# Attention in pairs of heads: one unit of two heads instead of one, with shared small operations

## The chip, the cores and the metric

The kernel runs on one core of one Trainium2 chip. The metric is the device time of one execution in microseconds, taken as the median of several runs. Lower is better.

## The reference

Two transformer blocks of two layers each, batch 1, 256 tokens, width 1024, all in fp32. The first block has four SwiGLU feed-forwards, an HGRN2 mixer and a forgetting attention of 16 heads. The second has a native sparse attention and a latent attention (12 heads each, plus 4 heads that look at 256 memory rows) and two mixtures of 16 experts. The change touches the attention of three stages, whose core is this, for each head:

```
# forgetting attention ("Fox"), scale = 1/sqrt(64), c = cumsum of log f
s = einsum('bhqd,bhkd->bhqk', qi, k) * scale + cqi[..., None] - c[:, :, None, :]
s = where(key_pos[None, :] <= qpos[:, None], s, MASK_VALUE)
o = einsum('bhqk,bhkd->bhqd', softmax(s), v)          # then o * sigmoid(g) @ w_out
# sparse attention ("Nsa"): o = gate0 * compressed + gate1 * selected + gate2 * window
# latent attention ("Mla"): heads of 64 + 32 columns in q and k, 64 in v, causal
# memory heads (in both): softmax(q mem_k^T / 8) mem_v, not masked
```

With 256 tokens the selected blocks and the window of the sparse attention are both the whole causal range, so each of its 12 heads has two causal softmaxes.

## The kernel before

Each engine's program is written out by hand, stage by stage, and the engines meet only at semaphores. The order of the stages is: FFN, HGRN2, FFN, FFN, Fox, FFN, Nsa, layer norm, mixture of experts, layer norm, Mla, layer norm, mixture of experts, layer norm. Weights come through a ring of three slots of 3 MB. Feed-forwards, projections and experts split each fp32 operand into two fp32r parts and multiply three times; attention multiplies in plain fp32, which the trace records as two records per matmul.

Class `Attention` (from line 1222) is shared by Fox, Nsa and Mla. Its piece of work is a **unit**: one head (in Nsa, one of the two softmaxes of one head) with all 256 queries in two tiles of 128. Fox has 16 units, Nsa 24 and 4 memory units, Mla 12 and 4. A causal unit has 256 keys for the second tile and 128 for the first, so 384 columns of scores; a memory unit has 512. The steps of a unit:

- `pe_score` (L1274): the scores of both tiles into one of four PSUM banks that go round (`banks.claim`). Fox adds a small fp32r product with the decay (`bias_rows`). The contraction is over 64 partitions, 0-63 for an even head and 64-127 for an odd one, and over 96 in Mla.
- `dve_score` (L1366): VectorE adds the mask, negates and takes the row extreme, from PSUM to one of four buffers `pr`.
- `act_units` (L1330): ScalarE makes the exponential of each tile in place, with its row sum.
- `dve_weight` (L1378): reciprocal of the sums, in Nsa times the gate, then one `tensor_scalar` per tile.
- `pe_turn` (L1283): TensorE transposes each 128x128 block of weights into PSUM bank 0 or 1, by turns.
- the copy (`copy_in`, L1318): ScalarE, or VectorE for every fourth unit (`copied_by_dve`, L1315), brings the turned weights to one of four buffers `pt` in the tile named squares.
- `pe_value` (L1298): times the values, 64 output partitions in bank 2 or 3, upper or lower half by the head.
- `dve_quarter` (L1396): after four heads, the bank goes to `cat`.

The order is a software pipeline with lags. At step s TensorE does scores s, turn s-2, values s-4; ScalarE the copy of s-3 and then the exponentials of s; VectorE reads the scores of s, weighs s-1, and copies s-3 if that is its own. The turn of unit g waits for the copy of unit g-2, whose bank it takes:

```
        if g >= 2:
            pe.wait_ge(k.att_copied[g % 2], g // 2)
        pe.wait_ge(k.att_scaled, g + 1)
```

In Nsa, `pe_before` (L1996) starts each pair of heads with one product over the compressed keys (L2008).

Of the kernel before, what the change touches and what calls it, by code (L numbers as in the profile page):

```python
# [24 lines left out]
P = 128  # L25
# [174 lines left out]
class Core:  # L200

    def __init__(self, ctx, nc, a):
# [63 lines left out]
        self.att_copied = [s("att_copied_0"), s("att_copied_1")]  # L267
        self.att_units = 0
        self.att_cols = f32("att_cols", [P, 3, 8])
# [952 lines left out]
class Attention(Mixer):  # L1222
# [6 lines left out]
    TURN_LAG, COPY_LAG, VALUE_LAG, DEEP = 2, 3, 4, 4  # L1229

    def plan_units(self, name, units, at):

        k, n = self.k, len(units)
        self.units, self.u0, self.name = units, k.att_units, name
        k.att_units += n
        part = lambda t: t.rearrange("p (r t) -> p r t", r=self.DEEP)
        self.pr, self.pt = part(at), part(k.sq[:].rearrange("p k t -> p (k t)"))
        self.quarter_end = [max(i for i, u in enumerate(units) if u["head"] // 4 == q) for q in range(4)]  # L1240
        self.quarter_start = [min(i for i, u in enumerate(units) if u["head"] // 4 == q) for q in range(4)]
        for i in range(n):
            k.banks.plan(f"{name}_s{i}")
# [19 lines left out]
    def pe_units(self, pe):  # L1263
        n = len(self.units)
# [33 lines left out]
    def pe_value(self, pe, j):  # L1298
        k, u, g = self.k, self.units[j], self.u0 + j
        q = u["head"] // 4  # L1300
# [17 lines left out]
    def copy_in(self, eng, j):  # L1318

        k, u, g = self.k, self.units[j], self.u0 + j  # L1320
        w = len(u["blocks"]) * P
# [8 lines left out]
    def act_units(self, act):  # L1330
        k, b, n = self.k, self.k.banks, len(self.units)
        for step in range(n + self.COPY_LAG):
            j = step - self.COPY_LAG
            self.act_before(act, step)
            if 0 <= j < n and not self.copied_by_dve(j):
                out, src, copied = self.copy_in(act, j)
                act.activation(out, src, ACT.Copy).then_inc(copied, 1)
            if step < n:
                u, r, c = self.units[step], step % self.DEEP, 2 * ((self.u0 + step) % 4)
                b.wait_read(act, f"{self.name}_s{step}")  # L1340
                for t, at, w in self.tiles(u):
                    e = self.pr[:, r, at:at + w]
                    act.activation(e, e, ACT.Exp, scale=-1.0, bias=k.att_cols[:, 0, c + t:c + t + 1],
                                   accum_out=k.att_cols[:, 1, c + t:c + t + 1]).then_inc(k.att_exp, 1)
        self.act_pieces(act, self.in_pieces + PIECES)

    def dve_units(self, dve):
        n, q = len(self.units), 0
        for step in range(n + self.COPY_LAG):
# [5 lines left out]
            if 0 <= j < n and self.copied_by_dve(j):  # L1355
                out, src, copied = self.copy_in(dve, j)
                dve.tensor_copy(out, src).then_inc(copied, 1)
# [8 lines left out]
    def dve_score(self, dve, i):  # L1366

        k, u, g, r, name = self.k, self.units[i], self.u0 + i, i % self.DEEP, f"{self.name}_s{i}"
        c = 2 * (g % 4)
        if i >= self.DEEP:  # L1370
            dve.wait_ge(k.att_turned, g + 1 - self.DEEP)
        src = k.banks.wait(dve, name)
        for t, at, w in self.tiles(u):
            ins = dve.tensor_tensor_reduce(self.pr[:, r, at:at + w], src[:, at:at + w], u["masks"][t], -u["scale"], -NEG_BIG, ALU.add,
                                           ALU.min, k.att_cols[:, 0, c + t:c + t + 1])
        k.banks.read(ins, name)

    def dve_weight(self, dve, j):  # L1378

        k, seq, u, g = self.k, self.k.dve_seq, self.units[j], self.u0 + j  # L1380
        c = 2 * (g % 4)
        total, weight = k.att_cols[:, 1, c:c + 2], k.att_cols[:, 2, c:c + 2]
# [1557 lines left out]
```

## Time and profile before

| | us |
|---|---|
| median of 3 runs | 2356.04 (2354.56 to 2358.23) |
| the profiled execution | 2355.3 |
| its span | 2353.2 |
| TensorE busy | 2178.4 (93%) |
| VectorE busy | 1527.5 (65%) |
| ScalarE busy | 1179.1 (50%) |
| mean granted TensorE clock | 0.952 of full speed |

### The profile page before, as it was taken

To read this page: it belongs to the slowest core of one execution; us is meant where nothing else is said; L and a number is where in the kernel's file an instruction comes from. 1 tells how busy PE (TensorE), PEld (TensorE's weight loads), DVE (VectorE), ACT (ScalarE), POOL (GpSimd) and SP (SyncE) were. 2 spreads that over 40 slices of the span, in tenths; PEclk is the share of its full clock that TensorE was granted. 3 is DMA by queue.
4 is the path that set the end of the run, shared out by engine and by line. 5 is a ranking of instruction groups with operands and counts; after the bars stand their busy time and mean duration, and the time that the engine had idled before them with its cause. 6 is when DMAs were issued, how large, how long until landed. Compare 5 with 4: busy or idle time off the path is not lost.

```text
span 2353.2 us, 36563 instructions
## 1 busy us (share of the span) xinstructions
PE 2178.4 (93%) x13974; PEld 1935.7 (82%) x13978; DVE 1527.5 (65%) x2373; ACT 1179.1 (50%) x1687; POOL 75.1 (3%) x55
## 2 busy tenths in 40 slices
PE   7998977999999989999999999799999898899997
PEld 6998966999999968779998876687788756778876
DVE  5665668666666544346564446589888455888985
ACT  4443543544434335435443335477776445676774
POOL 1000033000000010000000000000000000000000
PEclk9999998999999999769999969899999999899999
DMA  8545330454455532315545510489996513699991
GB/s 279 199 160 161 112 139 1 164 204 168 161 175 200 161 107 72 127 49 181 200 160 152 159 50 19 143 294 355 312 323 232 206 36 108 215 317 327 319 349 62
DMA packets 312312, 421.09 MB, mean 179 GB/s; under 512 B 7845, under 2 KB 266305, under 8 KB 312097
## 3 DMA queue, kind: packets, MB, share of 16 engines
q1 hardware_dynamic: 308864, 415.93, 52.1%
q10 hardware_dynamic: 2816, 2.38, 0.4%
q0 software_dynamic: 544, 1.62, 0.2%
q8 instruction: 54, 0.88, 0.2%
q14 instruction: 34, 0.27, 0.0%
HBM read 416.69 MB, written 1.05 MB: 178 GB/s over the span
## 4 chain that ended last, share of the span: by engine, by line
PE 84%; DVE 10%; ACT 3%; issue 2%; DMA 1%; ACTq 1%; POOL 0%; DVEq 0%; SPq 0%
PE banks L553 11%; PE banks L555 11%; PE banks L554 11%; PE banks L2493 7%; PE banks L2495 7%; PE banks L2494 7%; PE banks L805 5%; PE banks L806 4%; PE banks L807 4%; PE banks L1280 2%; PE banks L1310 2%; PE banks L2488 2%; PE banks L1289 1%; PE banks L2547 1%; DVE w_lo L2762 1%
## 5 line engine op out<-in xcount | busy, mean ns | idle before, releaser
L2762 DVE TENSOR_TENSOR w_lo<-weight_ring,w_hi 128x1024 fp32r<-128x1024 f32 x384 | 450.1, 1220 | 54.5 <-ACT w_hi L2607 51.1
L553 PE MATMUL banks<-x_hi,w_hi 128*128 128x256 f32 x1408 | 400.6, 284 | 9.0 <-DVE w_lo L506 8.3
L554 PE MATMUL banks<-x_lo,w_hi 128*128 128x256 f32 x1408 | 398.9, 283 | 0.0
L555 PE MATMUL banks<-x_hi,w_lo 128*128 128x256 f32 x1408 | 398.9, 283 | 0.0
L2607 ACT ACTIVATE w_hi<-weight_ring 128x1024 fp32r<-128x1024 f32 x384 | 381.4, 1052 | 33.8 <-PE banks L2495 33.8
L499 ACT ACTIVATE w_hi<-weight_ring 128x1024 fp32r<-128x1024 f32 x88 | 93.0, 1057 | 418.1 <-PE banks L555 418.0
L871 DVE TENSOR_TENSOR pieces<-weight_ring,pieces 128x512 fp32r<-128x512 f32 (+2 forms) x245 | 165.5, 687 | 191.6 <-ACT pieces L860 189.9
L553 PEld LDWEIGHTS banks<-x_hi,w_hi 128*128 128x128 f32 x1408 | 270.8, 192 | 11.3 <-DVE w_lo L506 9.1
L554 PEld LDWEIGHTS banks<-x_lo,w_hi 128*128 128x128 f32 x1408 | 270.9, 192 | 0.1
L555 PEld LDWEIGHTS banks<-x_hi,w_lo 128*128 128x128 f32 x1408 | 270.8, 192 | 0.0
L805 PE MATMUL banks<-split,pieces 128*128 128x256 f32 (+1 forms) x816 | 240.9, 295 | 28.0 <-DVE pieces L871 18.4
L860 ACT ACTIVATE pieces<-weight_ring 128x512 fp32r<-128x512 f32 (+2 forms) x245 | 150.7, 627 | 227.5 <-PE banks L807 217.1
L515 DVE TENSOR_TENSOR w_lo<-weight_ring,w_hi 128x1024 fp32r<-128x1024 f32 x88 | 107.8, 1225 | 240.1 <-ACT w_hi L499 240.1
L806 PE MATMUL banks<-split,pieces 128*128 128x256 f32 (+1 forms) x816 | 236.1, 289 | 0.0
L807 PE MATMUL banks<-split,pieces 128*128 128x256 f32 (+1 forms) x816 | 235.7, 289 | 0.0
L506 DVE TENSOR_TENSOR w_lo<-weight_ring,w_hi 128x2048 fp32r<-128x2048 f32 x88 | 201.2, 2286 | 22.2 <-ACT w_hi L495 21.9
L2493 PE MATMUL banks<-w_hi,x_hi 128*128 128x512 f32 x512 | 207.5, 405 | 2.0 <-ACT wide L2578 2.0
L2495 PE MATMUL banks<-w_lo,x_hi 128*128 128x512 f32 x512 | 201.7, 394 | 0.0
L2494 PE MATMUL banks<-w_hi,x_lo 128*128 128x512 f32 x512 | 200.9, 392 | 0.0
L553 PE MATMUL banks<-h_hi,w_hi 128*128 128x256 f32 x704 | 199.2, 283 | 0.0
L554 PE MATMUL banks<-h_lo,w_hi 128*128 128x256 f32 x704 | 199.2, 283 | 0.0
L555 PE MATMUL banks<-h_hi,w_lo 128*128 128x256 f32 x704 | 199.2, 283 | 0.0
(384 smaller groups left out, 4116.9 us busy)
## 6 DMA issues: line engine op xcount, KB each, us to landing
weight_ring<-in_ffn_w_in SPq DMA_DIRECT2D x88, 1024.0 KB, 7.5
weight_ring<-in_moe_w_gate SPq DMA_DIRECT2D x64, 1024.0 KB, 6.5
weight_ring<-in_moe_w_up SPq DMA_DIRECT2D x64, 1024.0 KB, 9.2
weight_ring<-in_moe_w_down SPq DMA_DIRECT2D x64, 1024.0 KB, 11.1
weight_ring<-in_ffn_w_out SPq DMA_DIRECT2D x44, 1024.0 KB, 9.7
weight_ring<-in_hg_w_in SPq DMA_DIRECT2D x12, 1024.0 KB, 8.3
weight_ring<-in_fox_w_in SPq DMA_DIRECT2D x12, 1024.0 KB, 8.4
weight_ring<-in_nsa_w_in SPq DMA_DIRECT2D x10, 1024.0 KB, 8.0
```

What stands on the lines that cost most here:

```text
L506: dve.tensor_tensor(k.w_lo[:, b, 0:2048].rearrange("p (k n) -> p k n", n=P), raw[:, 0:4096].rearrange("p (k n) -> p k n", n=256)[:, :, jj ...
L553: pe.matmul(out, w_hi, m_hi, start=start, stop=False, skip_group_check=True)
L554: pe.matmul(out, w_hi, m_lo, start=False, stop=False, skip_group_check=True)
L555: return pe.matmul(out, w_lo, m_hi, start=False, stop=stop, skip_group_check=True)
L805: pe.matmul(out, l_hi, r_hi, start=start, stop=False, skip_group_check=True)
L806: pe.matmul(out, l_hi, r_lo, start=False, stop=False, skip_group_check=True)
L807: return pe.matmul(out, l_lo, r_hi, start=False, stop=stop, skip_group_check=True)
L2493: pe.matmul(out, m_hi, w_hi, start=start, stop=False, skip_group_check=True)
L2494: pe.matmul(out, m_lo, w_hi, start=False, stop=False, skip_group_check=True)
L2495: return pe.matmul(out, m_hi, w_lo, start=False, stop=stop, skip_group_check=True)
L2607: act.activation(self.piece(s, p, self.w_hi), self.piece(s, p), ACT.Copy).then_inc(sem[kind + "_hi"], 1)
L2762: dve.tensor_tensor(self.piece(s, p, self.w_lo), self.piece(s, p), self.piece(s, p, self.w_hi.bitcast(F32)), ALU.subtract).then_inc(sem[ki ...
```

## The change

A unit becomes a pair of heads, the even one on partitions 0-63 and the odd one on 64-127. In Nsa a pair is the same softmax of two neighbouring heads, so its units are listed in another order. There are 8 pairs in Fox, 14 in Nsa, 8 in Mla.

- `pe_score` takes two banks and alternates the two heads' matmuls; `pe_value` alternates them too.
- `pe_turn` fills banks 0 and 1 with one pair and waits for the copy of the pair before it. There are no longer two banks by turns.
- One copy moves both heads, 2x384 or 2x512 elements. `pt` has two buffers of a pair in place of four of a unit, `pr` four of a pair (two of them in the first half of the tile wide).
- One reciprocal, one gate multiplication and one multiply per tile serve both heads. The multiply is a `tensor_tensor` with the weights broadcast along the row, in place of `tensor_scalar`.
- Values lag by 3 steps, not 4. ScalarE waits for the last turn before it goes on to the output projection's pieces.

```diff
-    TURN_LAG, COPY_LAG, VALUE_LAG, DEEP = 2, 3, 4, 4
+    TURN_LAG, COPY_LAG, VALUE_LAG, DEEP = 2, 3, 3, 4
...
     def pe_score(self, pe, i):
-        u, name = self.units[i], f"{self.name}_s{i}"
-        out = self.k.banks.claim(pe, name)
-        for t, at, n in self.tiles(u):
-            pairs = u["scores"][t]
-            for m, (left, right) in enumerate(pairs):
-                last = pe.matmul(out[:, at:at + n], left, right, start=m == 0, stop=m == len(pairs) - 1)
-        self.k.banks.filled(last, name)
+
+        k, pair = self.k, self.pairs[i]
+        outs = [k.banks.claim(pe, f"{self.name}_s{i}_{half}") for half in range(2)]
+        last = [None, None]
+        for t, at, n in self.tiles(pair[0]):
+            count = len(pair[0]["scores"][t])
+            for m in range(count):
+                for half in range(2):
+                    left, right = pair[half]["scores"][t][m]
+                    last[half] = pe.matmul(outs[half][:, at:at + n], left, right, start=m == 0, stop=m == count - 1)
+        for half in range(2):
+            k.banks.filled(last[half], f"{self.name}_s{i}_{half}")
 
     def pe_turn(self, pe, j):
-        k, u, g = self.k, self.units[j], self.u0 + j
-        if g >= 2:
-            pe.wait_ge(k.att_copied[g % 2], g // 2)
+        k, g = self.k, self.u0 + j
         pe.wait_ge(k.att_scaled, g + 1)
-        for m, (t, at) in enumerate(u["blocks"]):
-            last = pe.transpose(k.psum[:, g % 2, m * P:(m + 1) * P], self.pr[:, j % self.DEEP, at:at + P], k.ident)
+        if g:
+            pe.wait_ge(k.att_copied, g)
+        for half in range(2):
+            for m, (t, at) in enumerate(self.pairs[j][half]["blocks"]):
+                last = pe.transpose(k.psum[:, half, m * P:(m + 1) * P], self.pr[j % self.DEEP][:, half, at:at + P], k.ident)
         last.then_inc(k.att_turned, 1)
...
-        pe.wait_ge(k.att_copied[g % 2], g // 2 + 1)
-        half = u["head"] % 2 * HD
-        out = k.psum[half:half + HD, 2 + q % 2, u["head"] % 4 // 2 * T:(u["head"] % 4 // 2 + 1) * T]
+        pe.wait_ge(k.att_copied, g + 1)
+        out = k.psum[:, 2 + q % 2, head % 4 // 2 * T:(head % 4 // 2 + 1) * T]
         at = 0
-        for m, v in enumerate(u["values"]):
-            first, n = (T - u["spans"][m], u["spans"][m])
-            last = pe.matmul(out[:, first:T], v, self.pt[:, j % self.DEEP, at:at + n], start=m == 0 and u["first"],
-                             stop=m == len(u["values"]) - 1, skip_group_check=True)
+        for m, n in enumerate(pair[0]["spans"]):
+            for half in range(2):
+                last = pe.matmul(out[half * HD:(half + 1) * HD, T - n:T], pair[half]["values"][m], self.pt[:, j % 2, half, at:at + n],
+                                 start=m == 0 and pair[half]["first"], stop=m == len(pair[0]["spans"]) - 1, skip_group_check=True)
...
-        if j >= self.DEEP:
-            eng.wait_ge(k.att_out, g + 1 - self.DEEP)
-        return self.pt[:, j % self.DEEP, 0:w], k.psum[:, g % 2, 0:w], k.att_copied[g % 2]
+        if j >= 2:
+            eng.wait_ge(k.att_out, g - 1)
+        return self.pt[:, j % 2, :, 0:w], k.psum[:, 0:2, 0:w]
...
-        for t, at, w in self.tiles(u):
-            e = self.pr[:, j % self.DEEP, at:at + w]
-            ins = dve.tensor_scalar(e, e, k.att_cols[:, 2, c + t:c + t + 1], None, ALU.mult)
+        for t, at, w in self.tiles(pair[0]):
+            e = self.pr[j % self.DEEP][:, :, at:at + w]
+            ins = dve.tensor_tensor(e, e, weight[:, t].unsqueeze(2).to_broadcast([P, 2, w]), ALU.mult)
```

TensorE in the middle of Fox, before: one step. The arena operands are the heads' queries and keys, squares the turned weights.

```order
L1280 MATMUL banks<-arena 128x256 [waits bank_free_0]
L1280 MATMUL banks<-bias_rows 128x256
L1280 MATMUL banks<-arena 128x128
L1280 MATMUL banks<-bias_rows 128x128
L1289 MATMUL banks<-consts,arena 128x128 [waits att_scaled,att_copied_1]
L1289 MATMUL banks<-consts,arena 128x128 x2
L1310 MATMUL banks<-squares,arena 64x256 [waits att_copied_1]
L1310 MATMUL banks<-squares,arena 64x128
```

The same place in the changed kernel:

```order
L1288 MATMUL banks<-arena 128x256 [waits bank_free_2,bank_free_1]
L1288 MATMUL banks<-arena 128x256
L1288 MATMUL banks<-bias_rows 128x256 x2
L1288 MATMUL banks<-arena 128x128 x2
L1288 MATMUL banks<-bias_rows 128x128 x2
L1299 MATMUL banks<-consts,wide 128x128 [waits att_copied,att_scaled]
L1299 MATMUL banks<-consts,wide 128x128 x5
L1320 MATMUL banks<-squares,arena 64x256 [waits att_copied]
L1320 MATMUL banks<-squares,arena 64x256
L1320 MATMUL banks<-squares,arena 64x128 x2
```

A step holds two heads, and the turn waits on one semaphore that counts every copy, where it waited on the count of its own bank.

VectorE in Fox before, around the first copy that is its own (L1357): the copy of unit 3 stands between the multiply of unit 5 and the read of unit 7.

```order
L1374 ISA arena,att_cols<-banks,consts 128x256 [waits bank_ready_1,att_turned]
L1374 ISA att_cols 128x1
L1374 ISA arena,att_cols<-banks,consts 128x128
L1374 ISA att_cols 128x1
L1385 RECIPROCAL att_cols<-att_cols 128x2 [waits att_exp]
L1393 TENSOR_SCALAR arena<-arena,att_cols 128x256 [waits dve_seq]
L1393 TENSOR_SCALAR arena<-arena,att_cols 128x128
L1357 COPY squares<-banks 128x384 [waits att_turned]
```

And in the changed kernel, where the copy of pair 3 (L1369) stands behind the read of pair 6 and the multiply of pair 5:

```order
L1388 ISA wide,att_cols<-banks,consts 128x256 [waits bank_ready_3,att_turned]
L1388 ISA att_cols 128x1
L1388 ISA wide,att_cols<-banks,consts 128x128
L1388 ISA att_cols 128x1
L1388 ISA wide,att_cols<-banks,consts 128x256 [waits bank_ready_0]
L1388 ISA att_cols 128x1
L1388 ISA wide,att_cols<-banks,consts 128x128
L1388 ISA att_cols 128x1
L1399 RECIPROCAL att_cols<-att_cols 128x4 [waits att_exp]
L1407 TENSOR_TENSOR arena<-arena,att_cols 128x2x256 [waits dve_seq]
L1407 TENSOR_TENSOR arena<-arena,att_cols 128x2x128
L1369 COPY squares<-banks 128x2x384 [waits att_out,att_turned]
```

The position is the same, but what stands ahead of the copy is twice as much.

## Rows read from the trace of the kernel before

**Rows 1.** Windows, Fox, Nsa, Mla: length; PE, PEld, DVE, ACT, POOL busy; clock; DMA; GB/s.
```profile
974.74:1037.22 62.48, 61.02 (x208) 41.46 (x208) 25.21 (x121) 24.62 (x83) 0.00 (x0) 0.54 0.11 39
1382.46:1455.10 72.64, 70.54 (x328) 46.41 (x328) 48.93 (x239) 41.25 (x143) 0.00 (x0) 0.89 0.00 1
1914.80:1950.61 35.81, 33.73 (x180) 22.84 (x180) 26.26 (x122) 24.94 (x83) 0.00 (x0) 1.00 0.19 59
```
**Rows 2.** The chain that ended last, Fox: start us, us, what.
```profile
1007.21 1.90 PE banks L1280 x6
1009.10 0.83 PE banks L1289 x3
1009.93 1.47 PE banks L1310 x4
```
**Rows 3.** The same chain in Nsa, and the scores of a head in Mla.
```profile
1406.67 0.85 PE banks L1280 x4
1407.52 0.48 PE banks L1289 x3
1408.00 0.80 PE banks L1310 x4
...
1932.40 0.85 PE banks L1280 x4
```
**Rows 4.** Chain (first row), then timeline of TensorE: Fox's start, Mla's last values.
```profile
974.74 1.11 PE banks L1280 x6
...
976.62 0.30 PE L1280 MATMUL banks<-bias_rows 64*128 64x128 f32 x1
978.38 0.90 PE L1289 MATMUL banks<-consts,arena 128*128 128x128 f32 x3 [1.46 <-DVE arena L1393]
...
1947.07 1.08 PE L1310 MATMUL banks<-squares,arena 128*64 128x256 f32 x4
1948.67 1.94 PE L1310 MATMUL banks<-squares,arena 128*64 128x256 f32 x12
```
**Rows 5.** Timeline of a unit in Nsa: start us, us, engine, line, operation.
```profile
1437.07 0.42 DVE L1374 CUSTOM_DVE_ANT_0 arena<-banks,consts 128x256 f32<-128x256 f32 x1 [0.62 <-PE banks L1280]
1437.63 0.16 DVE L1387 RECIPROCAL att_cols<-att_cols 128x2 f32<-128x2 f32 x1
1438.02 0.55 DVE L1393 TENSOR_SCALAR arena<-arena,att_cols 128x256 f32<-128x256 f32 x2
1438.12 0.92 PE L1280 MATMUL banks<-arena 64*128 64x256 f32 x4
1439.18 0.42 DVE L1374 CUSTOM_DVE_ANT_0 arena<-banks,consts 128x256 f32<-128x256 f32 x1 [0.15 <-PE banks L1280]
1439.87 0.51 ACT L1343 ACTIVATE arena<-arena,att_cols 128x256 f32<-128x256 f32 x1 [0.76 <-DVE att_cols L1374]
1440.76 0.47 ACT L1337 ACTIVATE squares<-banks 128x384 f32<-128x384 f32 x1
```
**Rows 6.** Groups of instructions by shape, whole span: busy us, mean ns of one.
```profile
L871 DVE TENSOR_TENSOR pieces<-weight_ring,pieces 128x512 fp32r<-128x512 f32 x242 | 163.9, 689 | 188.7 <-ACT pieces L860 187.0
L529 DVE TENSOR_TENSOR slot_out<-banks,rstd 128x256 f32<-128x256 f32 x176 | 66.4, 419 | 21.0 <-PE banks L555 14.2
L1393 DVE TENSOR_SCALAR arena<-arena,att_cols 128x256 f32<-128x256 f32 x68 | 23.3, 352 | 2.1
L1393 DVE TENSOR_SCALAR arena<-arena,att_cols 128x128 f32<-128x128 f32 x52 | 14.6, 280 | 0.0
L1404 DVE COPY wide<-banks 128x512 f32<-128x512 f32 x8 | 5.5, 683 | 0.0
```
**Rows 7.** Windows behind Fox's last turns; columns as in rows 1.
```profile
1035.00:1037.00 2.00, 2.00 (x15) 1.23 (x13) 1.42 (x3) 1.88 (x4) 0.00 (x0) 0.76 0.00 0
1037.00:1039.00 2.00, 0.22 (x2) 0.00 (x0) 2.00 (x4) 0.42 (x1) 0.00 (x0) 1.00 0.00 0
1039.00:1042.00 3.00, 2.71 (x13) 2.74 (x14) 1.95 (x4) 0.21 (x1) 0.00 (x0) 0.56 0.00 0
```

More of the change, by code:

```diff
@@ L1263, in pe_units @@
     def pe_units(self, pe):
-        n = len(self.units)
+        n = len(self.pairs)
         for step in range(n + self.VALUE_LAG):
@@ L1298, in pe_value @@
     def pe_value(self, pe, j):
-        k, u, g = self.k, self.units[j], self.u0 + j
-        q = u["head"] // 4
+        k, pair, g = self.k, self.pairs[j], self.u0 + j
+        head = pair[0]["head"]
+        q = head // 4
         if q >= 2 and j == self.quarter_start[q]:
@@ L1330, in act_units @@
     def act_units(self, act):
-        k, b, n = self.k, self.k.banks, len(self.units)
+        k, b, n = self.k, self.k.banks, len(self.pairs)
         for step in range(n + self.COPY_LAG):
@@ L1355, in dve_units @@
             if 0 <= j < n and self.copied_by_dve(j):
-                out, src, copied = self.copy_in(dve, j)
-                dve.tensor_copy(out, src).then_inc(copied, 1)
+                out, src = self.copy_in(dve, j)
+                dve.tensor_copy(out, src).then_inc(k.att_copied, 1)
             if q < 4 and step - self.VALUE_LAG - 1 >= self.quarter_end[q]:
@@ L1366, in dve_score @@
     def dve_score(self, dve, i):
-        k, u, g, r, name = self.k, self.units[i], self.u0 + i, i % self.DEEP, f"{self.name}_s{i}"
-        c = 2 * (g % 4)
+        k, g = self.k, self.u0 + i
+        c = g % 4
         if i >= self.DEEP:
             dve.wait_ge(k.att_turned, g + 1 - self.DEEP)
[L1372 to L1376, printed above, removed]
-    def dve_weight(self, dve, j):
-        k, seq, u, g = self.k, self.k.dve_seq, self.units[j], self.u0 + j
-        c = 2 * (g % 4)
-        total, weight = k.att_cols[:, 1, c:c + 2], k.att_cols[:, 2, c:c + 2]
-        dve.wait_ge(k.att_exp, 2 * g + 2)
-        if u["gate"] is None:
+        for half, u in enumerate(self.pairs[i]):
+            name = f"{self.name}_s{i}_{half}"
+            src = k.banks.wait(dve, name)
+            for t, at, w in self.tiles(u):
+                ins = dve.tensor_tensor_reduce(self.pr[i % self.DEEP][:, half, at:at + w], src[:, at:at + w], u["masks"][t], -u["scale"],
+                                               -NEG_BIG, ALU.add, ALU.min, k.att_cols[:, 0, c, t, half:half + 1])
+            k.banks.read(ins, name)
+    def dve_weight(self, dve, j):
+        k, seq, pair, g = self.k, self.k.dve_seq, self.pairs[j], self.u0 + j
+        c = g % 4
+        total, weight = k.att_cols[:, 1, c], k.att_cols[:, 2, c]
+        dve.wait_ge(k.att_exp, 4 * g + 4)
+        if pair[0]["gate"] is None:
             seq.inc(dve.reciprocal(weight, total))
@@ L1388, in dve_weight @@
             seq.wait(dve)
-            seq.inc(dve.tensor_tensor(weight, total, u["gate"], ALU.mult))
+            seq.inc(dve.tensor_tensor(weight, total, pair[0]["gate"], ALU.mult))
         seq.wait(dve)
-        for t, at, w in self.tiles(u):
-            e = self.pr[:, j % self.DEEP, at:at + w]
-            ins = dve.tensor_scalar(e, e, k.att_cols[:, 2, c + t:c + t + 1], None, ALU.mult)
+        for t, at, w in self.tiles(pair[0]):
+            e = self.pr[j % self.DEEP][:, :, at:at + w]
+            ins = dve.tensor_tensor(e, e, weight[:, t].unsqueeze(2).to_broadcast([P, 2, w]), ALU.mult)
         ins.then_inc(k.att_scaled, 1)
@@ L1897, in __init__ @@
         units = []
-        for h in range(NSA_H):
-            pair, half, kv = h // 2, h % 2, h // GROUP
-            at = slice(half * HD, (half + 1) * HD)
-            vcol = slice(kv * HD, (kv + 1) * HD)
+        for pair in range(NSA_H // 2):
             for j, keys, v in ((1, self.ks, self.vs), (2, self.kw, self.vw)):
-                units.append(self.causal_unit(h, self.q[at, pair], keys[at, kv], [v[:, m, vcol] for m in range(TT)], HD ** -0.5,
-                                              gate=self.gates[:, :, 3 * h + j], first=False))
+                for half in range(2):
+                    h = 2 * pair + half
+                    at, vcol = slice(half * HD, (half + 1) * HD), slice(h // GROUP * HD, (h // GROUP + 1) * HD)
+                    units.append(self.causal_unit(h, self.q[at, pair], keys[at, h // GROUP], [v[:, m, vcol] for m in range(TT)], HD ** -0.5,
+                                                  gate=self.gates[:, :, 6 * pair + j:6 * pair + j + 4:3], first=False))
         self.plan_units("nsa", units + self.memory_units(), ar[:, 10240:12288])
@@ L1996, in pe_before @@
     def pe_before(self, pe, i):
-        k, h = self.k, self.units[i]["head"]
-        if h >= NSA_H or h % 2 or i != 2 * h:
+        k, h = self.k, self.pairs[i][0]["head"]
+        if h >= NSA_H or i % 2:
             return
```

45 lines of the change are left out of this document (26 added, 19 removed).

## The prediction

> **What bounds the kernel now.** I read the windows of the three attention stages first [rows 1]. They hold 62.5, 72.6 and 35.8 us, 171 us of the 2353.2 us span, and TensorE is busy in 165 of them. The thing to see is the clock column: 0.54 of full speed in Fox, 0.89 in Nsa, 1.00 in Mla. Then I read the chain that ended last, because a busy TensorE need not be what sets the end. In Fox it runs over TensorE alone, unit after unit, scores 1.90, turn 0.83, values 1.47 us [rows 2], sum 4.20 per head. In Nsa at full clock the same three cost 0.85, 0.48 and 0.80 [rows 3], sum 2.13; Mla's scores, over 96 partitions, take 0.85 too. So TensorE bounds all three stages, and Fox pays double because it runs at the lower level, 1.2 GHz, almost throughout. Before the clock fell TensorE had done four units' scores by 976.92 and then waited 1.46 us for the first multiply [rows 4]. The clock came back only when the last units' values ran one behind the other, 0.76 over 1035 to 1037 [rows 7].
>
> **Scores and values (pe_score, pe_value).** Nothing is removed from TensorE; the two heads' matmuls now stand side by side on different halves. Whether halves overlap is shown twice. Fox's first four units, whose heads alternate between partitions 0-63 and 64-127, take 1.11 us for one, but 2.18 us from the first record to the end of the last [rows 4], 1.09 per pair, against 2 x 0.95 (half of 1.90) one by one. The last three value units of Mla (12 records) take 1.94 us, 0.65 each, where one alone takes 1.08 [rows 4]: 0.60 of the time. So a pair costs: scores 1.1 in Fox, 0.95 in Nsa (2 x 0.85 x 0.57), 1.7 in Mla's 12 heads (96 rows leave no free half); values 0.95; turns 2 x 0.48 = 0.95. Bounds: full overlap gives scores of 0.85 to 0.95, none gives 1.7 to 1.9. TensorE then needs 3.0 us per pair in Fox, 2.85 in Nsa, 3.6 in Mla, against 4.26 (Nsa) now, and 8.4 in Fox at its clock.
>
> **VectorE.** Reading a unit's scores takes 0.56 us from start to start, the small column operations 0.39 with a gate [rows 5]. A pair's read is 1.12. The column operations are paid once per pair. The multiply becomes two tensor_tensor operations over 2x256 and 2x128; I price them by the rows for 512 and 256 elements, 0.69 + 0.42 = 1.11, where four tensor_scalar rows cost 2 x (0.35 + 0.28) = 1.26 [rows 6]. The weight work of a pair is then 0.39 + 1.11 = 1.5 (1.3 without the gate). The two tensor_scalar rows differ by 0.07 us over 128 elements, 0.56 ns each, the tensor_tensor rows by 1.05 ns each: the new form walks each element at half the pace and wins only by paying two starts for four. The Trainium skill, "VectorE: DVE Perf Modes", section "The perf-mode tier table", says exactly that tensor_scalar has a doubled rate for fp32 in SBUF and tensor_tensor has none. By that rule alone, which speaks against this edit and with which the two slopes agree, the multiply would cost 1.26 + 768 x 0.49 ns = 1.64, each long wait below 0.53 more, and the gain would be some 3 us smaller.
> The sum here goes by the whole rows. A copy of 2x384 is 0.68 + 256 x 1.05 ns = 0.95 [rows 6].
>
> **ScalarE.** Exponentials stay four per pair. A unit's two take 0.89 from start to copy, the copy 0.47 [rows 5]: 1.8 per pair, and 0.47 + 384 x 1.05 ns = 0.87 for the copy of 768 elements. Nothing is saved but one start.
>
> **The added wait.** Before, turns alternated between two PSUM banks, so a turn waited for the copy two units back. Now a pair's turn fills both banks, and pe_turn waits for the copy of the pair just before (att_copied >= g). Behind it stand the values of pair s-3 and the next scores. Two cases follow.
> Ordinary step, copy on ScalarE: from one copy's end turn 0.95, values 0.95, scores 0.95, then 0.2 to reach VectorE, 0.7 until the first exponential starts [rows 5], 1.8 of exponentials, copy 0.87: 6.4 us, over two steps, so 3.2 each.
> Every fourth pair VectorE copies, and there the copy of pair 3 stands behind read(6) and weight(5). After scores(6) TensorE waits 0.2 + 1.12 + 1.5 + 0.95 = 3.8 us; the step is 0.95 + 3.8 + 0.95 + 0.95 = 6.7. Today that copy is hidden behind a whole unit. Four Nsa steps: 3 x 3.2 + 6.7 = 16.3, against 8 x 2.13 = 17.0. The wait takes back most of what the halves give.
> These waits fall before turns 4, 8, 12 in Nsa and before turn 4 in Fox and Mla (pair 7 is last there, and its copy delays only the drain). Two microseconds of an almost idle TensorE are enough for a lower clock behind them: after 1037 to 1039, the next 3 us ran at 0.56 [rows 7]. I charge each long wait 1.6 us, half of such a 3 us stretch; the ends are 0 and 3.
>
> **Sum.** Fox: laid out in program order, scores(4) start at 10.3 us, two ordinary steps 6.5, the long step 6.5, last step and drain 9.8: 33.1 at full clock. The clock will fall at the start as today, since turn 0 comes even later (two reads, four exponentials, the multiply: 5.2 us after the start). It rose in Fox when values of even and odd heads ran side by side [rows 7], which every pair now does, so I expect it back some 10 us in: +3.5. One long wait: +1.6. Together 38.2 against 62.5: -24.3.
> Nsa: 57.1 by the same layout (10.3, twice 16, 3.6, drain 11.2); +5.6 for a start at the lower clock, +2.2 for five of the compressed products (L2008), +1.5 for the two wider memory pairs, +4.8 for three waits: 71.2 against 72.6: -1.4.
> Mla: 35.2, +1.0 memory pairs, +1.6: 37.8 against 35.8: +2.0.
> The end of each stage to the first output projection is the same work as before: cost nothing, all of it already behind the last copy; the new wait for att_turned ahead of it is over when it is reached. The ring of weights is full during attention (1 GB/s in Nsa [rows 1]), so nothing later waits for a load that it did not wait for. Sum -23.7. The profiled execution took 2355.3, which is 0.7 below the median of the three runs, 2356.0; I forecast **2332** for the median.
>
> **Rivals.**
> *A, forecast (0.57)*: Fox returns to full clock, long waits at the DVE copies. 2332, own range 2324 to 2341.
> *B (0.17)*: Fox overlaps its halves but stays at 1.2 GHz. For it: it stayed there for the whole stage while TensorE was 98% busy [rows 1]. Against: the rise at 1036 with heads side by side. A pair costs 2 x (1.90 x 0.57 + 0.83 + 1.47 x 0.60) = 5.6; eight and a drain of 4.7 are 49.5: -13. Total -12.4: 2343.
> *C (0.12)*: clock back at once and kept through the long waits: Fox 34, Nsa 66, Mla 36.5: -34.5, 2321. For it: Mla's clock is 1.00 over its whole window, the waits of its first steps included [rows 1]. Against: no row shows it kept through 3.8 us.
> *D, slower (0.06)*: the clock falls at the waits and stays low in all three stages. With TensorE at 1.85 times the warm cost, Nsa takes 89 (+16), Mla 54 (+18), Fox 49.5 (-13): +21, 2376. It decides if low stretches last over 15 us rather than the 3 us seen. The Trainium skill, "TensorE: Matmul & The Clock Gate", section "HAM oscillation", tells of just this, bursts parted by waits that bring the lower clock each time. Against it: the low stretch seen behind a pause ended once TensorE ran without a break [rows 7].
> *E, slower (0.04)*: the halves do not overlap, the change does not do what it says. TensorE keeps its 4.2 us per pair and five long waits of 3.8 come on top: +19, 2374. The rows of the four scores speak against it.
> *F, no change (0.04)*: B in Fox, and half of D's loss in one other stage: within 4.7 us.
>
> **How the numbers follow.** Faster by over 0.2% (4.7 us, about what measuring this kernel can tell from nothing) are A, B, C: 0.86. F is 0.04, D and E 0.10. The range 2315 to 2348 takes A, C and B with the bounds of overlap and of the clock, and leaves out D, E, F and the ends of B and C.
>
> **What would show it.** Fox's window: about 38 us, clock above 0.7 from some 990 us on; at 0.5 throughout, B. A turn at L1299 that waits near 3.8 us for the DVE copy at L1369, five times; if TensorE never waits above 1 us there, my long step is wrong. VectorE's L1407 near 690 and 420 ns; double those, and the skill's rule was the better guide. Nsa's and Mla's windows within 6 us of today's. Two heads' scores at full clock near 1.1 us in Fox; near 1.9, E. The forecast is wrong if any stage's clock does what no row here shows.

## The result and the profile after

The changed kernel takes 2322.4 us (median of 4 runs, 2318.8 to 2326.3) against 2355.4 (2354.6 to 2358.2) on the same chip: 0.9854 of the time, 95% interval 0.9839 to 0.9869. Faster, as forecast, and 10 us below the forecast time, at the figure of rival C. Its profiled execution took 2326.3 with a span of 2324.3, 28.9 below the span before. Beside the experiments further down, the kernel before took 2381 us in 3 of 11 executions (first group) and in 2 of 19 (second group); the ratios take these in, and by medians alone those of the first group are some 0.003 higher.

The windows of the three stages in the profile of the changed kernel, columns as in [rows 1]:

```profile
978.11:1011.12 33.01, 23.01 (x208) 17.19 (x208) 22.99 (x95) 22.20 (x75) 0.00 (x0) 0.95 0.21 74
1358.40:1422.38 63.98, 47.34 (x328) 32.86 (x328) 42.54 (x179) 38.14 (x130) 0.00 (x0) 0.85 0.00 1
1884.51:1920.72 36.21, 27.69 (x180) 20.17 (x180) 24.63 (x96) 23.28 (x76) 0.00 (x0) 0.91 0.19 59
```

Against [rows 1]: Fox goes from 62.48 to 33.01 and its clock from 0.54 to 0.95; Nsa from 72.64 to 63.98 at a slightly lower clock; Mla from 35.81 to 36.21. That is 37.7 us less in the stages. TensorE, busy 165 of 171 us before, is now busy 98 of 133, so in each of the three it waits for a good part of the time. The waits of TensorE, whole span (line waiting, line waited for: us in total, times, longest):

```profile
PE banks L1299 <- DVE squares L1369: 17.0, 5, 3.8
PE banks L1299 <- ACT squares L1347: 11.9, 13, 2.1
PE banks L1299 <- DVE arena L1407: 3.5, 3, 1.4
```

The five waits for VectorE's copy are the long steps of the forecast (3.51, 3.70, 3.70, 3.77 us, and 2.28 before Nsa's turn 12). Here is Fox's, TensorE's timeline (start us, us, line; in brackets the idle time and its releaser), and then VectorE's timeline in the same stretch:

```profile
994.12 0.70 PE L1288 MATMUL banks<-arena 64*128 64x256 f32 x4
994.92 0.30 PE L1288 MATMUL banks<-bias_rows 64*128 64x128 f32 x2
998.74 1.25 PE L1299 MATMUL banks<-consts,arena 128*128 128x128 f32 x6 [3.51 <-DVE squares L1369]
999.92 1.55 PE L1320 MATMUL banks<-squares,arena 128*64 128x256 f32 x8
1001.40 1.20 PE L1288 MATMUL banks<-arena 64*128 64x256 f32 x4
...
1002.93 0.88 PE L1299 MATMUL banks<-consts,arena 128*128 128x128 f32 x6
1003.73 0.87 PE L1320 MATMUL banks<-squares,arena 128*64 128x256 f32 x8
```

```profile
995.37 0.42 DVE L1388 CUSTOM_DVE_ANT_0 wide<-banks,consts 128x256 f32<-128x256 f32 x1 [0.61 <-PE banks L1288]
...
996.48 0.17 DVE L1399 RECIPROCAL att_cols<-att_cols 128x4 f32<-128x4 f32 x1
996.69 1.03 DVE L1407 TENSOR_TENSOR arena<-arena,att_cols 128x512 f32<-128x512 f32 x2
997.64 0.95 DVE L1369 COPY squares<-banks 128x768 f32<-128x768 f32 x1
```

Read, multiply, copy: exactly the three things that stood ahead of the turn in the order of the instructions. The first turn behind the wait takes 1.25 where the next takes 0.88, the first values 1.55 against 0.87: that is the clock. Windows of the changed kernel around the wait, columns as before, the clock the third number from the end:

```profile
994.00:998.50 4.50, 1.23 (x16) 0.92 (x12) 3.85 (x14) 2.21 (x10) 0.00 (x0) 1.00 0.01 2
998.50:1002.50 4.00, 3.76 (x20) 2.58 (x22) 0.09 (x1) 0.81 (x1) 0.00 (x0) 0.57 0.00 0
1002.50:1006.00 3.50, 2.10 (x24) 1.48 (x20) 2.83 (x12) 2.18 (x9) 0.00 (x0) 1.00 0.00 0
```

And the groups of the new shapes (busy us, mean ns of one), which answer to [rows 6]:

```profile
L1347 ACT ACTIVATE squares<-banks 128x768 f32<-128x768 f32 x20 | 15.9, 793 | 8.6 <-PE banks L1299 8.6
L1407 DVE TENSOR_TENSOR arena<-arena,att_cols 128x512 f32<-128x512 f32 x18 | 12.3, 691 | 0.5
L1407 DVE TENSOR_TENSOR arena<-arena,att_cols 128x256 f32<-128x256 f32 x14 | 5.8, 418 | 0.0
L1369 DVE COPY squares<-banks 128x768 f32<-128x768 f32 x6 | 5.7, 952 | 0.3 <-PE banks L1299 0.3
```

The stages give 37.7 us and the span 28.9. The other 8.8 us are lost outside of them: 3.4 before Fox, 2.0 and 2.4 between the stages, 1.0 behind Mla. Of the 2.4 behind Nsa, 0.7 is a later first matmul of the output projection (2.7 us behind the last values, 2.0 before), and the clock behind it is 0.66 over 1425 to 1430, where the same work ran at 1.00 before (1457 to 1462): this part belongs to the change. The largest piece lies between 355 and 425 us; first the kernel before, then the changed one, the same window:

```profile
355.00:425.00 70.00, 55.31 (x386) 50.46 (x385) 52.12 (x62) 21.70 (x27) 16.63 (x10) 0.88 0.03 8
```

```profile
355.00:425.00 70.00, 55.28 (x366) 50.23 (x366) 51.19 (x61) 20.57 (x25) 16.94 (x10) 0.83 0.00 1
```

The clock is lower, 20 fewer records of matmuls stand in the trace (some can be missing from a trace), and from there on everything is 2.4 us late. Of the thirteen profiles of this study, eleven start Fox's scores at 976.9 to 979.4 us and two (the kernel before, and one experiment) at 974.7 and 974.0, all with the same code up to there. What decides between them stays open; it is not the change. The time outside of the three stages was 2179 to 2198 us in the thirteen profiles, so a difference of a few us between two kernels is better read from the stages.

### The profile page after: what moved, and what is told of

Read it like the earlier page. It is cut to its first block, busy times and chain, and to the rows that moved or that the text cites. A ratio compares the mean times of both kernels' runs of the same rounds, so it can differ in the third digit from the quotient of the medians.

```text
span 2324.3 us, 36380 instructions
## 1 busy us (share of the span) xinstructions
PE 2120.3 (91%) x13978; PEld 1902.1 (82%) x13978; DVE 1518.1 (65%) x2263; ACT 1175.1 (51%) x1665; POOL 75.1 (3%) x55
## 4 chain that ended last, share of the span: by engine, by line
PE 82%; DVE 10%; ACT 4%; issue 2%; DMA 1%; ACTq 1%; POOL 0%; DVEq 0%; SPq 0%
PE banks L553 11%; PE banks L554 11%; PE banks L555 11%; PE banks L2507 7%; PE banks L2509 7%; PE banks L2508 7%; PE banks L805 5%; PE banks L806 5%; PE banks L807 5%; PE banks L2502 2%; PE banks L2561 1%; DVE w_lo L2776 1%; DVE pieces L871 1%; PE banks L1299 1%; DVE arena L1201 1%
```

## The experiments

All times are medians, ratios are to the kernel before on the same chip. The changed kernel was run once more beside the second group.

> The changed kernel as it is, once more on the same chip as the three others: 2319 to 2326, its Fox window 33 us, five waits of 2.3 to 3.8 us for VectorE's copy.

It took 2325.2 (ratio 0.9856, 0.9815 to 0.9898), stages 32.9, 65.3 and 36.2 us.

**Is the wait for VectorE's copy what is left?** Two ways to take it away. All copies on ScalarE:

```diff
     def copied_by_dve(self, j):
-        return j % 4 == 3
+        return False
```

> The changed kernel with every copy of turned weights on ScalarE, none on VectorE. Theory W (the waits for VectorE's copy and the slow clock behind them are what is left of the cost): the five waits at the turn, 17.0 us together in the changed kernel's profile, go, a long step of 6.7 us becomes an ordinary one of 3.2 to 3.4, and the 1.9 us of slow clock behind each go too: 5 x 3.3 + 4 x 1.9 = 24 us, 2298. Rival S (ScalarE takes the place): the copy's 0.79 us comes on top of ScalarE's 1.8 us of exponentials, waits for its copy grow by about as much, gain under 8 us, 2315 or more.

And the copy first in VectorE's step:

```diff
         for step in range(n + self.COPY_LAG):
+            j = step - self.COPY_LAG
+            if 0 <= j < n and self.copied_by_dve(j):
+                out, src = self.copy_in(dve, j)
+                dve.tensor_copy(out, src).then_inc(k.att_copied, 1)
             if step < n:
                 self.dve_score(dve, step)
             if 1 <= step < n + 1:
                 self.dve_weight(dve, step - 1)
-            j = step - self.COPY_LAG
-            if 0 <= j < n and self.copied_by_dve(j):
...
```

> The changed kernel, VectorE still copies every fourth pair, but as the first thing of its step, ahead of the read and the multiply. Theory W: the turned weights stand ready then, so the wait of 3.5 to 3.8 us goes and only the copy's 0.95 us, which now lies ahead of the read, may show: 24 - 5 x 0.9 = 20 us, 2302. Rival: the wait is the sum of VectorE's work wherever the copy stands, gain under 5 us.

Measured: 2302.2 (0.9736, 0.9686 to 0.9786) and 2303.3 (0.9739, 0.9689 to 0.9789). The windows of the first, all copies on ScalarE:

```profile
978.66:1006.40 27.74, 21.43 (x208) 16.30 (x208) 20.61 (x92) 22.66 (x75) 0.00 (x0) 1.00 0.25 88
1352.98:1406.03 53.05, 43.89 (x328) 30.75 (x328) 39.80 (x176) 39.73 (x133) 0.00 (x0) 0.89 0.00 1
1868.21:1898.21 30.00, 24.64 (x180) 18.32 (x180) 21.98 (x92) 23.68 (x76) 0.00 (x0) 1.00 0.22 71
```

110.8 us in place of 133.2, and Fox's and Mla's clock is 1.00. Theory W gave 2298 and 2302: the five waits and the clock behind them cost 20 us (23 against the second run of the changed kernel), a little less than the 24 expected. Where VectorE copies matters little as long as nothing stands ahead of the copy. Rival S falls: the waits for ScalarE's copy only went from 11.9 to 14.9 us.

**The copy between the exponentials.** What remained were 14.9 us of waits for ScalarE's copy, because the copy stands ahead of both heads' exponentials one step late. Here it stands between them, one step earlier:

```diff
-        for step in range(n + self.COPY_LAG):
-            j = step - self.COPY_LAG
+        for step in range(n + self.TURN_LAG):
+            j = step - self.TURN_LAG
...
-            if 0 <= j < n and not self.copied_by_dve(j):
-                out, src = self.copy_in(act, j)
-                act.activation(out, src, ACT.Copy).then_inc(k.att_copied, 1)
-            if step < n:
...
-                for half in range(2):
+            for half in range(2):
+                if half and j >= 0:
+                    out, src = self.copy_in(act, j)
+                    act.activation(out, src, ACT.Copy).then_inc(k.att_copied, 1)
+                if step < n:
```

> All copies on ScalarE, and each stands between the exponentials of the two heads of a pair, one step earlier than now, so that it has ended before TensorE wants the next turn. Theory W with the remaining 0.8 to 1.4 us waits for ScalarE's copy gone as well: a step costs what TensorE needs, 2.6 to 2.8 us, so Fox 27, Nsa 54, Mla 31: about 20 us under the changed kernel from the long waits, 12 more from the short ones, 2290. Rival S: ScalarE at 2.6 us per pair and VectorE at 2.4 to 2.8 are as full as TensorE and the step stays at 3.2, 2300.

2296.5 (0.9707, 0.9656 to 0.9758), the stages:

```profile
977.70:1003.05 25.35, 21.46 (x208) 16.30 (x208) 20.52 (x92) 22.55 (x75) 0.00 (x0) 1.00 0.27 95
1351.53:1400.75 49.22, 44.12 (x328) 30.87 (x328) 39.62 (x176) 39.75 (x133) 0.00 (x0) 0.88 0.00 1
1863.17:1890.78 27.61, 24.47 (x180) 18.29 (x180) 21.82 (x92) 23.56 (x76) 0.00 (x0) 1.00 0.23 77
```

102.2 us, another 8.6 less; the time is 5.7 less, between the 2290 and the 2300 of the two theories, with the stages a little below the 27, 54 and 31 of theory W. TensorE's waits for ScalarE's copy fall to 1.6 us. With the next experiment's variant of it, this is the fastest version, about 26 us under the change.

**The multiply alone.** The same kernel with four tensor_scalar in place of two tensor_tensor:

```diff
         for t, at, w in self.tiles(pair[0]):
-            e = self.pr[j % self.DEEP][:, :, at:at + w]
-            ins = dve.tensor_tensor(e, e, weight[:, t].unsqueeze(2).to_broadcast([P, 2, w]), ALU.mult)
+            for half in range(2):
+                e = self.pr[j % self.DEEP][:, half, at:at + w]
+                ins = dve.tensor_scalar(e, e, weight[:, t, half:half + 1], None, ALU.mult)
```

> The kernel with the copy between the exponentials, and the multiply again as four tensor_scalar operations per pair, 2 x (0.35 + 0.28) = 1.26 us, in place of two tensor_tensor, which measure 0.69 + 0.42 with 1.03 from start to end. If VectorE is not what sets a step there, the time stays within 3 us of 2296; if it is, each of the 30 pairs costs 0.23 more, 2303. The rule that tensor_tensor walks 768 elements at half the pace of tensor_scalar would have it 1 to 10 us faster instead.

2294.4 (0.9728, 0.9689 to 0.9767), no difference that these runs can tell. (The profiled execution, 2283.0, was the shortest of six; the others took 2292 to 2296.) A pair of heads on VectorE's timeline, four tensor_scalar:

```profile
985.52 1.01 DVE L1408 TENSOR_SCALAR wide<-wide,att_cols 128x256 f32<-128x256 f32 x4
```

1.01 us against the 1.03 of two tensor_tensor above. The durations of the four add up to 1.26, but instructions that need not wait for each other overlap; start to end, both forms cost the same. Sharing the multiply gave nothing that these runs can tell. That the time stayed within 3 us does not show, as the expectation has it, that VectorE is not what sets a step: the 0.23 us that were to tell it are not there.

**Do the halves keep the clock up?** First the order within a pair, all of head 0's matmuls ahead of head 1's:

```diff
-        for t, at, n in self.tiles(pair[0]):
-            count = len(pair[0]["scores"][t])
-            for m in range(count):
-                for half in range(2):
+        for half in range(2):
+            for t, at, n in self.tiles(pair[0]):
+                count = len(pair[0]["scores"][t])
+                for m in range(count):
```

and the same two loops exchanged in pe_value.

> The changed kernel, but the matmuls of a pair's first head all stand ahead of those of its second, in scores and in values; everything else stays. A pair of scores should then take 1.7 to 1.9 us at full clock and values 1.6, against 1.0 and 0.87 alternated. Theory T (the halves side by side are what keeps the clock up in Fox): Fox's clock falls to near 0.55 again and its window goes from 33 to 55 us or more, Nsa and Mla lose clock too; 2365 to 2380. Rival G (it is the grouping into pairs, the pattern of waits, that keeps the clock): Fox keeps 0.9 or more and takes 8 x 1.4 = 11 us more, 44; Nsa about 12 more, Mla 4 more; 2349.

2323.4 (0.9829, 0.9779 to 0.988): as the changed kernel, and neither theory's time. The premise was wrong. A pair of scores of Nsa on TensorE's timeline, here and, second, in the changed kernel:

```profile
1390.97 0.93 PE L1288 MATMUL banks<-arena 64*128 64x256 f32 x8
```

```profile
1392.99 0.92 PE L1288 MATMUL banks<-arena 64*128 64x256 f32 x8
```

Eight records, which are four fp32 matmuls, in 0.93 us, as alternated, where one head's four records took 0.85 in [rows 3]. So heads in turn overlap as well. The records of the scores in the first 0.10 us of such a stretch (busy of PE and PEld, clock, DMA, GB/s), here and, second, for a head alone in the kernel before:

```profile
1390.97:1391.07 0.10, 0.10 (x2) 0.10 (x2) 1.00 0.00 0
```

```profile
1406.60:1406.70 0.10, 0.10 (x1) 0.10 (x1) 1.00 0.00 0
```

Two records run at once from the start, although the whole first head stands ahead in the program. At two matmuls per head adjacency is enough. With four per head (six records, two of them of the decay), in Fox, a pair took 1.6 in place of 1.1. That is what the kernel before shows at Fox's start: three heads in 2.18 us, each starting 0.54 behind the one before, the last alone 1.09.

To part the halves, other work must stand between them. From the kernel with the copy between the exponentials:

```diff
-            if step < n:
-                self.pe_score(pe, step)
-            self.pe_after_score(pe, step)
...
+            for half in range(2):
+                if step < n:
+                    self.pe_score(pe, step, half)
+                if half:
+                    self.pe_after_score(pe, step)
+                if 0 <= step - self.TURN_LAG < n:
+                    self.pe_turn(pe, step - self.TURN_LAG, half)
+                if 0 <= step - self.VALUE_LAG < n:
+                    self.pe_value(pe, step - self.VALUE_LAG, half)
```

> The kernel with the copy between the exponentials, but TensorE takes head 0's scores, head 0's turn, head 0's values and then the same of head 1, so that two heads' matmuls never stand next to each other and no two halves can work together. Everything else, copies and waits included, stays. At full clock a pair then costs 2 x 0.95 + 0.88 + 1.6 = 4.3 us. Theory T (halves working together are what keeps the clock up in Fox): Fox's clock falls to near 0.55 and its window goes from 25 to 60 us or more, Nsa to 70, Mla to 36: about 2360. Rival G (it is the pattern of waits and the units of two heads): Fox keeps 0.9 or more and takes 8 x 4.3 + 6 = 40, Nsa 66, Mla 36: about 2336.

2364.8 (1.0035, 1.0006 to 1.0065; executions from 2351 to 2381): as theory T, which said 2360, and nothing of the gain is left. Its windows: Fox, a piece of its start, its middle, then Nsa and Mla:

```profile
977.31:1033.65 56.34, 54.35 (x208) 36.88 (x208) 21.34 (x92) 23.41 (x75) 0.00 (x0) 0.61 0.12 43
978.00:982.00 4.00, 2.57 (x29) 2.32 (x27) 3.26 (x19) 3.44 (x14) 0.00 (x0) 1.00 1.08 371
986.00:1020.00 34.00, 34.00 (x107) 23.02 (x106) 10.46 (x48) 10.74 (x37) 0.00 (x0) 0.50 0.00 0
1382.41:1462.95 80.54, 76.50 (x328) 49.43 (x328) 41.01 (x176) 41.39 (x133) 0.00 (x0) 0.80 0.00 1
1924.92:1962.29 37.37, 33.64 (x180) 22.72 (x180) 22.57 (x92) 24.44 (x76) 0.00 (x0) 1.00 0.17 57
```

The pairs, the shared operations and the copies are those of the fastest kernel, and so is the arithmetic; the first pause is 1.74 us in place of 1.42. Fox entered at full clock, fell to the lower level and stayed there for 34 us in which TensorE was busy all the time. This is the kernel before once more [rows 1, 2]. Mla is different: it kept a clock of 1.00 with the halves apart, as in the kernel before.

Then one overlap at a time. Values apart, the scores of both heads together:

```diff
+            if 0 <= step - self.VALUE_LAG < n:
+                self.pe_value(pe, step - self.VALUE_LAG, 0)
             if step < n:
                 self.pe_score(pe, step)
             self.pe_after_score(pe, step)
+            if 0 <= step - self.VALUE_LAG < n:
+                self.pe_value(pe, step - self.VALUE_LAG, 1)
             if 0 <= step - self.TURN_LAG < n:
                 self.pe_turn(pe, step - self.TURN_LAG)
...
```

> The kernel with the copy between the exponentials, with only the values of the two heads kept apart: head 0's values, both heads' scores (alternating), head 1's values, both turns. A pair costs TensorE 1.1 + 0.88 + 1.6 = 3.6 us at full clock in Fox. Theory T in a weak form (one of the two overlaps is enough to keep the clock in Fox): Fox at 0.9 or more, 8 x 3.6 + 4 = 33 us, all stages 102 + 8 x 0.7 + 14 x 0.7 + 8 x 0.7 = 123, 2317. Theory T in its strong form (both are needed): Fox at 0.6, near 48 us or more, 2335.

and scores apart, in the same way, with both heads' values between them.

> The same kernel with only the scores kept apart: head 0's scores, both heads' values (alternating), head 1's scores, both turns. TensorE needs 1.9 + 0.88 + 0.87 = 3.65 us per pair in Fox at full clock. Weak form: Fox at 0.9 or more, 33 us, 2317. Strong form: Fox at 0.6, near 48 us or more, 2335. If only one of the two kernels keeps the clock, it is that overlap (scores, which fill the rows, or values, which fill the columns) that counts.

Measured: 2336.3 (0.9912, 0.9897 to 0.9927) and 2370.1 (1.0063, 1.0049 to 1.0077). Fox, a piece of it, and Nsa, values apart:

```profile
977.45:1015.88 38.43, 28.39 (x208) 20.45 (x208) 20.72 (x92) 22.88 (x75) 0.00 (x0) 0.91 0.18 63
984.00:990.00 6.00, 5.28 (x22) 3.54 (x23) 2.43 (x12) 2.53 (x9) 0.00 (x0) 0.50 0.00 1
1363.74:1430.58 66.84, 53.53 (x328) 35.84 (x328) 40.10 (x176) 40.19 (x133) 0.00 (x0) 0.91 0.00 1
```

and scores apart (this profile took 2354.8, one of two short executions; the other five took 2367 to 2372 at a lower mean clock, 0.933 to 0.937 in place of 0.942, and no trace of them is kept), Fox, Nsa, Nsa's middle:

```profile
978.73:1010.36 31.63, 27.27 (x208) 21.57 (x208) 20.96 (x92) 23.19 (x75) 0.00 (x0) 1.00 0.22 76
1356.47:1452.96 96.49, 90.83 (x328) 60.70 (x328) 41.03 (x176) 41.33 (x133) 0.00 (x0) 0.51 0.00 1
1370.00:1430.00 60.00, 60.00 (x212) 40.16 (x208) 24.48 (x110) 23.38 (x78) 0.00 (x0) 0.50 0.00 1
```

For Fox the weak form holds, in two ways. With the scores apart the clock never fell; with the values apart it fell behind the first pause, stayed at 1.2 GHz for some 7 us and came back. The times are far above the 2317 of the weak form, because Nsa (66.8 and 96.5) and, with the values apart, Mla (39.0, in place of 27.6) took much longer than costed; Mla's 39.0, at a clock of 1.00, was not followed up. Nsa does not follow the theory. It begins at 1.2 GHz in every kernel, and with the scores apart it never left it. With both parted it did leave it, late (0.80 over the stage). So staying at full clock and getting back to it may be two things. Which order of TensorE's work brings it back is not settled by these runs.

**The overlap alone.** The kernel before with only TensorE's order changed: two units at a time, scores and values alternating, two turns between (Nsa's units in the order of the pairs):

```diff
-        for step in range(n + self.VALUE_LAG):
+        for step in range(0, n + self.VALUE_LAG, 2):
             if step < n:
                 self.pe_score(pe, step)
+            for s in (step, step + 1):
...
+                if 0 <= s - self.TURN_LAG < n:
+                    self.pe_turn(pe, s - self.TURN_LAG)
```

> The kernel before, with one part of the change alone: TensorE takes two units at a time, their scores alternating, then their two turns, then their values alternating, and Nsa's units stand in the order of the pairs. VectorE and ScalarE keep single heads, the turn keeps its two banks, four buffers and the copy two units back. Theory O (TensorE's halves and the clock are the whole gain, the shared operations and the shared turn buffer are its cost): Fox 30, Nsa 55, Mla 32, no wait over 1 us for a copy by VectorE, 2302 or less, as fast as the changed kernel with all copies on ScalarE. Rival P (VectorE's work per head, 1.57 us in Fox and 1.75 in Nsa, bounds it at 3.1 to 3.5 us per pair and the shared operations are needed): 2313 or more.

The same with all copies on ScalarE:

> The kernel before with TensorE taking two units at a time, now with all copies on ScalarE. If the 40 us of waits for VectorE's copy in the run with two units were the price of that copy standing behind a read and a multiply, they go and the three stages take 149 - 25 to 35: 2308 to 2315, and what is then left over against the pairs with all copies on ScalarE (110.8 us in the stages) is what the shared operations save. If the shared operations are what counts, most of the wait turns into waits for the multiply and the gain is under 8 us, 2331 or more.

2339.2 (0.9918, 0.9889 to 0.9948) and 2334.4 (0.991, 0.9895 to 0.9926). Fox and Nsa of the first, then its waits at the turn (L1295 here, the copy is L1365, the multiply L1401), then those of the second:

```profile
977.87:1011.37 33.50, 22.75 (x208) 16.18 (x208) 24.44 (x121) 23.50 (x82) 0.00 (x0) 1.00 0.21 73
1357.74:1436.14 78.40, 56.83 (x328) 35.80 (x328) 47.80 (x239) 41.00 (x143) 0.00 (x0) 0.77 0.00 1
```

```profile
PE banks L1295 <- DVE arena L1401: 20.9, 20, 1.7
PE banks L1295 <- DVE squares L1365: 18.6, 12, 1.7
```

```profile
PE banks L1295 <- DVE arena L1401: 35.3, 32, 1.7
```

Fox's whole gain is there with TensorE's order alone (62.5 to 33.5, clock 1.00). Nsa is not faster but slower (78.4): TensorE waits at every pair, and its clock is 0.77. Rival P was the right one, and in the second run the wait for the copy turned into one for the multiply, as its other branch said. (I wrote 40 us for the waits for the copy in that expectation; that figure counted the weight loads' idle time as well, the row says 18.6.) The second run's stages take 32.2, 66.7 and 35.8 us, 134.8 against 149.1 in the first, while the rest of its span is 7 us longer: in the three stages TensorE's order with all copies on ScalarE gives what the change gives (133.2; the profiled executions differ by 8 us, 6.6 of it outside of the stages). The pairs are worth their cost only once VectorE's copy no longer stands behind a read and a multiply: with all copies on ScalarE they take 110.8, 24 us less than single heads, and 32 us less in all (2302.2 against 2334.4). Most of the 24 lies in Nsa (13.7) and Mla (5.8). Which part of a pair it is, the one copy, the one hand-over for two heads or the shared small operations, was not separated; only the multiply is excluded.

## Why the prediction was right, and where not

The forecast was 2332, range 2315 to 2348, faster with 0.86. The time is 2322.4: inside the range, sign right, 10 us too high.

- **What bounds it, halves overlap**: right, but the row behind its size was misread. The window of the kernel before that holds Fox's first scores shows 18 records, six to a head, so three heads, where I counted four:

```profile
974.00:978.00 4.00, 2.18 (x18) 1.92 (x18) 1.59 (x10) 3.42 (x10) 0.00 (x0) 0.99 1.10 361
```

2.18 us for three is 0.73 each, 1.45 per pair and not 1.09; the factor 0.57 behind Nsa's 0.95 and rival B's 5.6 comes from the same count. No row of the kernel before shows an alternated pair of Fox. That it then took 1.10 is luck. Pairs of scores take 1.1 in Fox and 0.92 in Nsa, values 0.87 (0.95 said), turns 0.88. The halves-apart run shows that without the overlap nothing is gained.
- **VectorE and ScalarE**: read 1.11 (1.12 said), multiply 1.03 (1.11), VectorE's copy 0.952 (0.95), ScalarE's 0.79 (0.87). The two shapes of L1407 are 691 and 418 ns, the two rows I had taken them from. I had the tensor_scalar form too dear: 1.26 is the sum of durations that overlap, and start to end it is 1.01; [rows 5] already gave 0.55 for two in a row. So "wins by paying two starts for four" is wrong, it wins nothing. The tier table of the Trainium skill ("VectorE: DVE Perf Modes") orders the two forms per element as the rows do, but the sum built on it, 1.64, was 0.6 above the 1.03 measured.
- **The long wait**: right in kind, place and size. 3.8 said; 3.51, 3.70, 3.70 and 3.77 measured, and 2.3 at Nsa's turn 12, which I had also charged 3.8 although no read stands ahead of that copy. The clock fell behind each of the four waits of 3.5 to 3.8 us, for some 3.4 us each; in Fox turn, values and scores then took 0.37, 0.68 and 0.5 more, 1.55 together, 1.6 said. My "two microseconds are enough" is not borne out as a rule: behind 1.92 us in Fox and 2.28 in Nsa the clock did not fall, behind 2.07 in Mla it did.
- **Ordinary step** 3.2: near, Fox's were 4.0, 2.6 and 3.6, 3.4 in the mean.
- **Fox** 38.2 said, 33.0 measured. The step that failed is "the clock will fall at the start as today", +3.5: it was 1.00 until the long wait, through pauses of 1.42 and 1.32 us. The pause before the first multiply [rows 4], which I took for the cause of the fall, is there in both kernels, 1.46 and 1.42 us. In the kernel before the clock was 0.50 from the end of that pause on; in the changed kernel it did not fall; with the values apart it fell and came back; with the halves apart it fell and stayed. So heads kept apart make the fall last in Fox, and what starts it stays open. The remaining 1.7 us are steps laid out a little too long.
- **Nsa** 71.2 said, 64.0 measured; **Mla** 37.8 and 36.2. The mechanism was right, sizes were not. From Nsa's start to scores(4) 14.2 us in place of 15.9, four steps with a long one (from turn 4 to turn 8) 17.1 in place of 18.5, and the drain with its shorter wait some 3 less.
- **The rest of the span** was costed at nothing. In the profile it gave back 8.8 us, so that the stages (37.7) were 14 us better than my 23.7 while the span was 5 better. That the first output projection costs nothing more did not hold behind Nsa, as shown above. A forecast of 2332 came closer than its parts deserved.
- **Rivals**: B (Fox stays at 1.2 GHz) did not happen, but it is what happens when the halves are parted. C comes nearest in its figures, 2321 and 34, 66 and 36.5 for the stages, but of its mechanism only the first half held: the clock was kept at Fox's start, and through none of the four longest waits. D, E and F did not happen. E's premise, halves that do not work together, was built as an experiment and came out at 2365 where I had said 2374.

## What to carry to other kernels

When operations are shared over two units, look at which buffer they now fill together: a wait for "the one just before" exposes everything that stands ahead of its copy on the copying engine. Put that copy first, or into a gap of an engine with room, here worth 20 to 26 us on top of the 33 of the change. For matmuls that fill half of the array, place two independent halves next to each other in TensorE's program, and judge a busy TensorE by its granted clock before its busy share.

## What was not expected of the hardware

- A TensorE that is busy without a gap can stay at 1.2 GHz: 34 us with the halves apart in Fox, 60 us in Nsa with the scores apart, 100% busy in both windows above.
